# Value products right behind the scores of a later group, in all eight attentions of a fused two-stack transformer kernel

## The reference, cut to what matters

```python
# first stack, layer 0: forget-gate attention (8 heads) + sparse attention (8 heads, three branches)
s = q @ k.T * scale + (cq - c_k);  p = masked_softmax(s, causal);  o = p @ v
o = g0 * o_compressed + g1 * o_selected + g2 * o_window
# first stack, layer 1: differential attention, 8 heads of value width 128
p = a1 - lam * a2;  o = rms_norm(p @ v, subln_g) * (1 - lam_init)
# both layers then: x += cross attention to 256 memory tokens (4 heads); x += swiglu
# second stack, both layers: x += 0.5 swiglu; then three branches, mixed by gates:
#   neighbourhood attention (8 heads), gated linear attention, latent attention (4 heads, value width 128)
mixed = gt0 * (y_na @ w_na) + gt1 * (y_gla @ w_gla) + gt2 * (y_mla @ w_mla);  x += mixed @ w_out; x += 0.5 swiglu
```

## Time and profile before

| what | value |
|---|---|
| runs of the kernel | 2175.52 us median of 3 (2170.46, 2175.52, 2176.01) |
| the profiled execution: its time | 2171.44 us |
| the profiled execution: span of the trace | 2169.5 us |
| mean clock granted to TensorE | 0.976 of full |
| instructions | 26737 |
| PE busy | 2060.2 us (95%) |
| DVE busy | 1253.9 us (58%) |
| ACT busy | 1044.5 us (48%) |
| mean HBM rate | 159 GB/s |

### The profile page before, as it was taken

One profiled execution on the slowest core, in us unless ns is written; L12 is line 12 of the kernel. 1 busy time (PEld: TensorE's weight loads), 2 busy tenths in 40 slices (PEclk: granted clock), 3 DMA queues, 4 the chain that ended last, 5 costly groups with the idle time before them and its releaser, 6 DMA issues. The chain is left out here.

```text
span 2169.5 us, 26737 instructions
## 1 busy us (share of the span) xinstructions
PE 2060.2 (95%) x9920; PEld 1679.9 (77%) x9932; DVE 1253.9 (58%) x1812; ACT 1044.5 (48%) x1661; POOL 141.7 (7%) x146
## 2 busy tenths in 40 slices
PE   6988799999889999999999999999999999899999
PEld 6765688877668888888777788888888777778887
DVE  4646654466765556455656765455555574766554
ACT  5544544455554445445455545445444456555433
POOL 0000000000000000000302200000000212120000
PEclk9988999999989999999999999999999999999999
DMA  7420465554235555554452545555555453435552
GB/s 265 150 98 21 136 198 188 184 187 141 78 116 186 190 185 179 183 193 163 134 187 64 175 156 175 190 180 177 191 194 178 140 194 103 136 121 171 186 193 98
DMA packets 247640, 346.12 MB, mean 160 GB/s; under 512 B 28180, under 2 KB 177496, under 8 KB 247512
## 3 DMA queue, kind: packets, MB, share of 16 engines
q1 hardware_dynamic: 246680, 342.92, 48.9%
q0 software_dynamic: 544, 1.29, 0.3%
q10 hardware_dynamic: 288, 0.21, 0.0%
HBM read 343.32 MB, written 2.33 MB: 159 GB/s over the span
## 5 line engine op out<-in xcount | busy, mean ns | idle before, releaser
L473 DVE TENSOR_TENSOR w_lo<-raw,w_hi 128x2048 fp32r<-128x2048 f32 (+5 forms) x486 | 740.6, 1543 | 411.9 <-ACT w_hi L485 411.4
L644 PE MATMUL bank<-w_hi,h_hi 128*128 128x512 f32 (+3 forms) x1904 | 752.2, 395 | 40.9 <-ACT h_hi L1368 15.4
L485 ACT CAST w_hi<-raw 128x2048 fp32r<-128x2048 f32 (+5 forms) x486 | 618.9, 1301 | 261.3 <-PE bank L646 260.2
L646 PE MATMUL bank<-w_hi,h_lo 128*128 128x512 f32 (+3 forms) x1904 | 738.8, 388 | 0.0
L645 PE MATMUL bank<-w_lo,h_hi 128*128 128x512 f32 (+3 forms) x1904 | 737.8, 388 | 0.0
L644 PEld LDWEIGHTS bank<-w_hi,h_hi 128*128 128x128 f32 x1904 | 363.4, 191 | 121.7 <-ACT w_hi L485 11.2
L646 PEld LDWEIGHTS bank<-w_hi,h_lo 128*128 128x128 f32 x1904 | 363.3, 191 | 71.2
L645 PEld LDWEIGHTS bank<-w_lo,h_hi 128*128 128x128 f32 x1904 | 364.0, 191 | 65.4
L644 PE MATMUL bank<-w_hi,ff_hi 128*128 128x512 f32 x528 | 206.0, 390 | 0.0
L646 PE MATMUL bank<-w_hi,ff_lo 128*128 128x512 f32 x528 | 205.5, 389 | 0.0
L645 PE MATMUL bank<-w_lo,ff_hi 128*128 128x512 f32 x528 | 205.5, 389 | 0.0
(11 more groups left out here) (290 smaller groups left out, 1673.4 us busy)
## 6 DMA issues: line engine op xcount, KB each, us to landing
raw<-in_ffn_w SPq DMA_DIRECT2D x176, 512.0 KB, 4.6
raw<-in_w_in SPq DMA_DIRECT2D x52, 1024.0 KB, 5.2
raw<-in_ffn_w SPq DMA_DIRECT2D x44, 1024.0 KB, 4.9
raw<-in_ffn_wg SPq DMA_DIRECT2D x44, 512.0 KB, 4.0
raw<-in_ffn_wu SPq DMA_DIRECT2D x44, 512.0 KB, 5.0
raw<-in_ffn_wd SPq DMA_DIRECT2D x22, 1024.0 KB, 4.9
raw<-in_od_w_in SPq DMA_DIRECT2D x12, 1024.0 KB, 5.1
raw<-in_w_out SPq DMA_DIRECT2D x8, 1024.0 KB, 5.1
```

Of the source, the lines that this page charges most:

```text
L473: dve.tensor_tensor(lo_[:, cs], raw_[:, cs], hi[:, cs].bitcast(F32), ALU.subtract).then_inc(*dve_did.up())
L485: act.copy(hi[:, cs], raw_[:, cs]).then_inc(*act_did.up())
L644: pe.matmul(out, x_hi, u.hi[:, k, cols_], start=start, stop=False)
L646: return pe.matmul(out, x_lo, u.hi[:, k, cols_], start=False, stop=stop)
```

## The change

In every pass of the loop in `attention` the value products of group i-1, together with their exit from PSUM, are issued directly behind the scores of group i+2, and the second portion of side work comes after them. Nothing else is moved, added or taken out.

```diff
                 begin(i + 2)
                 if i < len(groups):
                     normed(i)
-                fill(b)
                 if i >= 1:
                     summed(i - 1)
+                fill(b)
             turn["gentle"] = False
             attended["o"] = marks()
```

## The result

The changed kernel takes 2176.07 us in the median of 20 runs (2172.74 to 2183.25), the kernel before 2171.65 us in the median of 20 (2167.08 to 2179.37). The ratio is 1.0022, 95% interval 1.0013 to 1.0032: slower by some 4.8 us (2.8 to 6.9). Forecast were +3.2 us, and no change beyond 0.3%. Both hold for the ratio. But the interval reaches only 0.1% to either side and leaves out 1: the change is small, and against the forecast it can be told from none. The forecast time, 2178.7 us, is 2.6 us above the measured one, because it was put on the median of the first three runs, which lies 3.9 us above that of the twenty.

What follows compares the result with a forecast made beforehand. PE was taken as the bound, busy 2060.2 of 2169.5 us. The terms 0.5 + 1.3 + 0.4 + 1.0 = +3.2 us, put on the median 2175.52, gave 2178.7 us, range 2171 to 2186.

Steps and rivals of the forecast that it cites:

- No wait to remove in the second stack: Neighbourhood and latent attentions: PE stays covered in both orders, cost 0 (at most 0.7 us), gain 0.
- Layer 0, +0.5: Layer 0, passes 1 and 2: a DVE chain starts later, net 0.46 us, all reaching PE; taken as +0.5 us.
- The bound of -1.1: Layer 0's lower bound: earlier exits of groups 2 and 3 might remove a PE wait of 1.11 us; not counted.
- Differential, pass 2, +1.3: Differential attention, pass 2 to 3: ACT's chunk exit and DVE's list behind it move 1.33 us later; bounds 0 to 2.0.
- The bank wait: Differential attention, transposes of group 2: they wait for ACT's 0.69 us chunk exit from their bank, hidden inside another wait.
- Pass 5, +0.4: Differential attention, pass 5: squares on ACT come behind the exit, so DVE's sums wait, +0.4 us; bounds 0 and 1.15.
- Pass 8, +1.0: Differential attention's end: second four transposes fall behind the last value products, output projection starts 1.0 us later; bounds 0 and 1.5.
- Sum, +3.2: Whole kernel: the terms of layer 0 and of differential passes 2, 5 and 8 together, +3.2 us.
- rival 2: Slower by clock: half clock for half of the differential attention's 24 us, 4.6 us more, together +7.8, 2183.3 us; chance 0.16.
- rival 3: Faster by clock: earlier products keep the clock up in layer 0, -6.2 us, 2169.3 us; chance 0.07.

Runs made afterwards that it cites:

- e9: Kernel before with the exchange made in the neighbourhood and latent attentions alone; ratio 0.9997 (0.9988 to 1.0006).
- e10: Kernel before with the exchange made in layer 0 alone; ratio 1.0007 (0.9995 to 1.0018).
- e8: Changed kernel, but in the differential attention the transposes of group 2 take the next PSUM bank; stage 61.14 us, as in the changed kernel.
- e3: Kernel before with the exchange made in pass 2 of the differential attention alone; stage 60.82 us against 58.57, value products of group 6 +1.34 us.
- e4: Kernel before with the exchange made in pass 5 of the differential attention alone; stage 58.90 us, +0.33.
- e5: Kernel before with the exchange made in pass 8, the last, of the differential attention alone; stage 59.48 us, +0.91.
- e1: Kernel before with the exchange made in all passes of the differential attention, nowhere else; ratio 1.0025 (1.0012 to 1.0038), stage 61.13 us against 58.57.
- e2: Kernel before with the exchange made in all attentions but the differential one; ratio 1.0006 (0.9994 to 1.0018), stage 58.60 us.

## Why the prediction was right

- **No wait to remove in the second stack**: right. e9 measures 0.9997. The copy on DVE stood before the value products in the changed kernel (ended 1265.94, products 1266.57), a margin of 0.6 us against the 0.5 forecast, here the two rows:

```profile
1265.26 0.68 DVE L1053 COPY gain<-bank 128x512 f32<-128x512 f32 x1
```
```profile
1266.57 1.89 PE L1091 MATMUL bank<-gain,z 128*128 128x256 f32 x8
```

- **Layer 0, +0.5**: wrong at its end. The 0.46 arise as worked out, +0.44 at L1948 and +0.43 at the scores of the fifth group (e10). I put them into the sum in full, because PE idles ahead of these scores in any case; but the next transposes are only 0.19 late, DVE's copy behind them is 1.02 early, and at the output projection -0.04 (e10 against the kernel before) or +0.16 (e8 against e3). The bound of -1.1 had such a payback in it, at another wait; I didn't count it.
- **Differential, pass 2, +1.3**: 1.34 by e3. The value products of group 1 had covered ACT's exit of the chunk; moved ahead of the side work they cover nothing. The bank wait was forecast at 0.69 and hidden; it is 0.78 and hidden (e8). Together the two waits are 2.21 us where 2.4 were forecast.
- **Pass 5, +0.4**: 0.33 by e4, through the place named: L1102 ahead of L2195, and DVE's sums behind both.
- **Pass 8, +1.0**: 0.91 by e5. I had put 0.26 us between the last L635 and the first product, after it lies about 0.1.
- **Sum, +3.2**: the terms as measured give 2.57 and at most 0.16, about 2.6 to 2.7. The whole is +4.8 (2.8 to 6.9). So some 2 us are without an owner in the stages, and that 3.2 lies inside the interval is in part luck: 0.5 of it did not last, and what the timed runs add is not in it. As far as the intervals tell, the rest goes with the exchange in the differential attention (e1 1.0025, e2 1.0006), yet e1's own trace ends that stage at +2.56. Less clock in the mean doesn't explain it: runs with a mean clock of 0.976 have a median of 2171.3 us before (20 runs made beside the experiments), 2175.7 in the changed kernel (11) and 2176.9 in e1 (5). Where in the kernel the clock falls could still do it, as one such fall cost 0.9 us in e3, but no trace here tells how often that happens in the timed runs. This stays open.
- **Rivals**: rival 2 as put (half of the 24 us at half clock) and rival 3 did not happen: clock 1.00 in 546 to 571.5, and 0.78 and 0.79 in 126 to 209. The one fall inside the stage, in e3, cost 0.9 us and not the 4.6 that I gave rival 2.

The Trainium skill, page "TensorE: Matmul & The Clock Gate", section "HAM oscillation", was cited for rival 2: idle gaps between bursts put the clock back. The runs here bear it out only in part: in e3 the clock falls once, behind waits of at most 1.43 us, while the changed kernel, e1 and e8, with the same two waits and more idle behind them, show no fall in this stage.

## What to carry to other kernels

Where lists run in order, an instruction that PE does late has a second use: it gives ACT and DVE time to empty a bank. Before moving products "to be done sooner", ask what they cover where they stand and who waits for the result; here nobody waited for the outputs, and three places lost their cover (1.34, 0.33 and 0.91 us in e3, e4 and e5). A delay can also be paid back further on, as in layer 0, so follow it to the end of its stage before it goes into the sum. Where whole times scatter by 0.3%, compare the distance between two landmarks in a stage that ran at full clock; it repeated within 0.05 us over these traces (58.56 to 58.60 in five with the order of before, 61.13 and 61.14 in three with the changed one). Where the clock moves, compare only traces in which it moves alike.

## What the runs showed of the hardware that I had not expected

The granted clock of one stretch is not fixed by the instructions: 0.97, 0.91, 0.95 and 0.91 in the same 100 us of work, with 0.91 under either order (e5 has the order of before there). And the part of the kernel up to the first transposes of the differential attention, with the same old order in layer 0, took 504.38 us in e3, 504.68 in e9 and 509.82 in e1. Of the 5.4 us between e3 and e1, 4.2 are there at the first transposes of layer 0 already (82.38 and 86.55), where the two kernels are the same: the granted clock in 42 to 52, 52 to 62 and 62 to 75 us is 0.83, 1.00 and 1.00 in e3, and 1.00, 0.83 and 0.87 in e1.
